# Prompt attention of a hybrid decoder step: two heads of a token block in one turn, each pair in its own half of the TensorE array

## The chip, the cores and the metric

The kernel runs on one core of one Trainium2 chip. Everything is 32-bit floating point. The metric is the device time of one execution in microseconds, from the first to the last instruction of the program and what lies around them; three executions were timed, and a further one was profiled.

## The reference, cut to what matters

Two layers, each with three token mixers side by side (a gated linear recurrence, a state-space mixer, dilated attention), a merge, and a channel mixer (dense in layer 0, eight experts in layer 1). 256 prompt tokens and 32 sample tokens go through the same weights. The change touches the prompt half of the attention: 4 heads of 64 features, three groups of projections (dilations 1, 4 and 16), whose keys lie together in one softmax.

```python
s = jnp.einsum('bnqrhd,bnkrhd->bnrhqk', qb, kb, preferred_element_type=jnp.float32) * ATT_SCALE
s = jnp.where(valid[None, :, None, None], s, -jnp.inf)
m = jnp.max(s, axis=-1, keepdims=True)
p = jnp.exp(s - m)
den = jnp.sum(p, axis=-1, keepdims=True)
o = jnp.einsum('bnrhqk,bnkrhd->bnqrhd', p, vb) / jnp.transpose(den, (0, 1, 4, 2, 3, 5))
```

So for every head and every block of 128 query tokens: scores (a contraction over 64 features), a softmax over the row, and a product of the weights with the values (64 features out).

## The kernel before, in words

Features lie on partitions, tokens in columns. TensorE is written out by hand as one long list of products; each product goes to one of eight PSUM banks, and a planning pass (`plan_mixer`) says which bank each product fills and in which order a bank is filled. `open_bank` makes TensorE wait until the bank's last content has been taken out, and `close_bank` signals that it is full. VectorE (DVE) and ScalarE (ACT) take banks out in their own hand-written orders. SyncE issues all weight and cache loads.

**Units.** The prompt attention of a layer is eight units, n = 0 to 7: unit n is head n // 2 and query block n % 2. The first block sees one block of keys, the second two. A unit goes like this:

- `scores(L, n, k)` (TensorE): for key block k three products (one for each group) of 64 partitions into bank 0. Heads 0 and 2 lie on partitions 0 to 63, heads 1 and 3 on 64 to 127.
- `prompt_scores` (DVE, from L2579): L2588 scales and masks each bank of scores into the buffer `sc`, L2591 takes the row maximum, L2592 negates it. ACT exponentiates with a running sum, DVE takes the reciprocal (L2603) and scales the row (L2604).
- `turn_weights(L, n, k)` (TensorE): three transposes of the weights into bank 2, copied out by ACT into `PT`.
- `weigh(L, n)` (TensorE): for each key block three products of 128 partitions with 64 output features, into partitions 0 to 63 or 64 to 127 of bank 4.

**Between them** stand other products of the same TensorE list. `sample_keys(L, n, k)` turns the cached keys of sample sequence n in four parts, into banks 5 and 6; DVE copies out parts 0 and 1 (L2599, L2601), ACT parts 2 and 3. `sample_scores` (one for every two sequences) needs all eight parts and runs in four column quarters of the array. `out_tile(br, m)` is one tile of the other mixers' output projections, into bank 1, taken out by DVE in `gated` (a L2284 instruction). The turning of unit n's weights and its value products stand in turn n + 1, behind the next unit's scores and key turns.

All of TensorE's products are recorded at L974 (`put`) and all of its transposes at L980 (`turn`); in the trace a product of 32-bit numbers is two records and a transpose is one. A record's shape is written partitions*columns of the loaded weights, then the output: 64*128 are the scores, 128*64 the value products, 128*32 the sample scores, 128*128 with 288 columns an `out_tile` product. ACT's instructions stand at L1838.

Of the kernel before, what the change touches and what calls it, by code (L numbers as in the profile page):

```python
# [84 lines left out]
def hybrid_decoder(nc, x_prompt, x_sample, state_hgrn, state_ssm, state_conv, cache_kv_w128, cache_kv_w512,  # L85
# [6 lines left out]
    with ctx:  # L92
# [140 lines left out]
        sc = [view(arena, 16128, 1, 384), view(arena, 16512, 2, 384)]  # L233
        PT = [view(arena, 17280, 1, 384), view(arena, 17664, 2, 384)]
# [99 lines left out]

        def plan_mixer(L):
# [79 lines left out]
            for n in range(9):  # L415
                if n < 8:
                    for k in range(n % 2 + 1):
                        job(("sc", L, n, k), 0)
                    if n == 0:
                        job(("sS", L, 0), 7)  # L420
                        job(("sS", L, 1), 3)
# [4 lines left out]
                if n > 0:  # L426
                    for k in range((n - 1) % 2 + 1):
                        job(("pt", L, n - 1, k), 2)
                    if (n - 1) % 4 == 0:
                        job(("att_o", L, (n - 1) // 4), 4)  # L430
# [525 lines left out]
        def _(pe):  # L956
# [421 lines left out]
            def weigh(L, n):  # L1378
                h, tb = n // 2, n % 2
                j, r = h // 2, 64 * (h % 2)  # L1380
                key = ("att_o", L, j)
                acc = open_bank(key) if n % 4 == 0 else psum(key)
                for k in range(tb + 1):
                    pe.wait_ge(*drained(("pt", L, n, k)))
# [6 lines left out]
                if n % 4 == 3:  # L1391
# [136 lines left out]
            def mixer(L):  # L1528
# [26 lines left out]
                for n in range(9):  # L1555
                    if n < 8:
                        scores(L, n, 0)
                        sample_keys(L, n, 0)
                        if n % 2:
                            scores(L, n, 1)  # L1560
                        sample_keys(L, n, 1)
                    if n > 0:
                        turn_weights(L, n - 1, 0)
                    if n < 8:
                        out_tile(0, n)
                        sample_keys(L, n, 2)
                        sample_keys(L, n, 3)
                        if n % 2:
                            out_tile(1, n // 2)
                    if n > 0 and n % 2 == 0:  # L1570
                        turn_weights(L, n - 1, 1)
                        sample_scores(L, n // 2 - 1)
                    if n > 0:
                        weigh(L, n - 1)
# [242 lines left out]
        def _(act):  # L1817
# [148 lines left out]
            def attention(L):  # L1966
# [5 lines left out]
                def turned_weights(m, k):  # L1972
                    key = ("pt", L, m, k)
                    copy_out(PT[m % 2][:, k, :], key, psum(key)[:, 0:384])

                for n in range(9):
                    if n < 8:
                        w = n % 2 + 1
                        act.wait_ge(*at("sc_neg", L, n + 1))
# [1075 lines left out]
```

## Time and profile before

| | us |
|---|---|
| three executions | 2180.27, 2180.68, 2182.74 (median 2180.68) |
| the profiled execution | 2180.18 |
| its span, first to last instruction | 2178.4 |
| TensorE busy (matmul) | 2137.6 (98%) |
| DVE busy | 602.9 (28%) |
| ACT busy | 376.9 (17%) |
| granted TensorE clock, mean | 0.996 |

A record's busy time runs to its modelled end. Matmul records overlap, so what an item costs on TensorE is read from its start to the start of the next item. The two layers' attention stretches run from 376.25 and from 1125.72 us of the span; the expert stage of layer 1 takes the time from about 1292 us to the end.

### The profile page before, as it was taken

What the parts mean: (1) busy time and instruction counts of PE and PEld (TensorE: products, weight loads), DVE (VectorE), ACT (ScalarE), POOL (GpSimd) and SP (SyncE); (2) the same over time, 40 slices, a digit from 0 to 9 for tenths busy, and PEclk for the clock granted to TensorE, in tenths of its full rate; (3) what the DMA queues carried; (4) which work ended last, traced back from release to release, by engine and by line L of the source; (5) the groups of instructions that cost most, each with busy time, mean ns of one, the idle gap of its engine ahead of it and who ended that gap; (6) DMA issues with size and microseconds to landing.
All of it is one profiled execution on the core that took longest, in us unless ns stands there. A gap on an engine that the chain in (4) does not pass through costs nothing.

```text
span 2178.4 us, 43348 instructions
## 1 busy us (share of the span) xinstructions
PE 2137.6 (98%) x19425; PEld 1330.8 (61%) x19425; DVE 602.9 (28%) x1181; ACT 376.9 (17%) x676; POOL 101.2 (5%) x150
## 2 busy tenths in 40 slices
PE   7999999999999999999999999999999999999998
PEld 6777777777777777777776753434343434343434
DVE  5395333443110124933244321010101010101013
ACT  3323424311000023243333030000000000000000
POOL 2001020000000000011200010000000000000001
PEclk9999999999999999999999999999999999999999
DMA  5434535684443453354464859999999999999996
GB/s 161 135 99 141 157 119 159 178 258 135 137 136 101 133 176 117 117 161 128 129 190 130 290 215 406 417 404 416 405 416 404 417 404 415 397 413 398 413 411 238
DMA packets 298648, 548.64 MB, mean 252 GB/s; under 512 B 12665, under 2 KB 229115, under 8 KB 282016
## 3 DMA queue, kind: packets, MB, share of 16 engines
q1 hardware_dynamic: 290476, 535.85, 68.3%
q10 hardware_dynamic: 6644, 5.58, 0.8%
q0 software_dynamic: 1344, 4.45, 0.5%
q8 instruction: 153, 2.51, 0.5%
q14 instruction: 31, 0.25, 0.0%
HBM read 527.15 MB, written 22.50 MB: 252 GB/s over the span
## 4 chain that ended last, share of the span: by engine, by line
PE 94%; DVE 3%; DMA 2%; ACT 1%; issue 1%; ACTq 0%; DVEq 0%
PE bank L974 92%; PE bank L980 2%; DMA mem<-in_w_moe_down_dram 1%; ACT mem L1838 1%; DVE mem L2588 0%; DVE col L2591 0%; DVE mem L2559 0%; DVE mem L2601 0%; DVE mem L2604 0%; ACTq L2148 0%; DMA hv<-in_ssm_d_dram 0%; DVE mem L2284 0%; DVE mem L2599 0%; ACT L1838 0%; DVE mem L2280 0%
## 5 line engine op out<-in xcount | busy, mean ns | idle before, releaser
L974 PE MATMUL bank<-mem 128*32 128x256 f32 (+10 forms) x11936 | 999.9, 403 | 19.2 <-DVE mem L2284 5.7
L974 PEld LDWEIGHTS bank<-mem 128*32 128x32 f32 (+3 forms) x11936 | 566.1, 121 | 434.3 <-issue 233.5
L974 PE MATMUL bank<-hflat,mem 128*128 128x288 f32 (+1 forms) x2944 | 716.6, 406 | 1.3 <-ACT hflat L1838 0.7
L974 PEld LDWEIGHTS bank<-hflat,mem 128*128 128x128 f32 (+1 forms) x2944 | 538.1, 188 | 163.3 <-issue 19.4
L1838 ACT ACTIVATE mem<-bank 128x288 f32<-128x288 f32 (+6 forms) x347 | 158.8, 463 | 802.4 <-PE bank L974 763.5
L974 PE MATMUL bank<-mem,steps 128*32 128x384 f32 (+1 forms) x3072 | 289.8, 539 | 0.0
L974 PEld LDWEIGHTS bank<-mem,steps 128*32 128x32 f32 x3072 | 95.3, 110 | 191.2 <-issue 190.3
L2284 DVE SCALAR_TENSOR_TENSOR hflat<-hflat,bank 128x512 f32<-128x512 f32 x24 | 15.1, 683 | 411.3 <-ACT hflat L1838 411.3
L1838 ACT ACTIVATE hflat<-bank 128x512 f32<-128x512 f32 (+1 forms) x40 | 19.6, 554 | 569.1 <-PE bank L974 546.2
L2284 DVE SCALAR_TENSOR_TENSOR mem<-mem,bank 128x288 f32<-128x288 f32 (+1 forms) x93 | 43.2, 479 | 214.4 <-ACT mem L1838 178.3
L1838 ACT ACTIVATE mem<-mem 128x1152 f32<-128x1152 f32 (+9 forms) x105 | 83.4, 796 | 100.1 <-DVE mem L2358 71.6
L2280 DVE TENSOR_TENSOR mem<-mem 128x1152 f32<-128x1152 f32 (+6 forms) x101 | 87.5, 867 | 7.4 <-ACT mem L1838 2.4
L980 PE MATMUL bank<-ident,mem 128*128 128x128 f32 (+3 forms) x459 | 65.2, 281 | 12.5 <-DMA mem<-in_x_sample_dram 7.4
L980 PEld LDWEIGHTS bank<-ident,mem 128*128 128x128 f32 (+3 forms) x459 | 52.6, 145 | 25.5 <-issue 12.2
L2287 DVE SCALAR_TENSOR_TENSOR mem<-mem,bank 128x384 f32<-128x384 f32 (+1 forms) x45 | 21.4, 505 | 168.0 <-PE bank L974 168.0
L1838 ACT ACT_TABLE_LOAD x41 | 52.6, 1283 | 15.3 <-issue 11.3
L930 POOL DMA_INDIRECT mem<-yslots,mem x6 | 5.9, 978 | 836.4 <-PE bank L974 834.9
L2287 DVE SCALAR_TENSOR_TENSOR hflat<-hflat,bank 128x512 f32<-128x512 f32 x24 | 15.1, 683 | 78.9 <-PE bank L974 78.9
L1838 ACT ACTIVATE hflat<-xT 128x288 f32<-128x288 f32 x24 | 10.6, 443 | 141.0 <-DVE xT L2280 86.3
L1838 ACT ACTIVATE mem<-mem,col 128x384 f32<-128x384 f32 (+2 forms) x18 | 14.7, 814 | 78.2 <-DVE col L2592 75.3
L2588 DVE SCALAR_TENSOR_TENSOR mem<-bank,amask 128x384 f32<-128x384 f32 x24 | 13.4, 558 | 50.8 <-PE bank L974 50.8
L2437 DVE SCALAR_TENSOR_TENSOR mem<-mem,vecs 128x312 f32<-128x312 f32 x48 | 26.1, 545 | 1.7
(239 smaller groups left out, 707.2 us busy)
## 6 DMA issues: line engine op xcount, KB each, us to landing
mem<-in_w_moe_up_dram SPq DMA_DIRECT2D x64, 2048.0 KB, 21.3
mem<-in_w_moe_down_dram SPq DMA_DIRECT2D x56, 2048.0 KB, 21.7
mem<-in_w_moe_up_dram SPq DMA_DIRECT2D x32, 2304.0 KB, 23.1
mem<-in_w_in_dram SPq DMA_DIRECT2D x70, 1024.0 KB, 5.2
mem<-in_w_moe_up_dram SPq DMA_DIRECT2D x16, 1536.0 KB, 22.2
mem<-in_w_ffn_up_dram SPq DMA_DIRECT2D x44, 512.0 KB, 4.8
mem<-in_cache_kv_w_dram SPq DMA_DIRECT2D x26, 512.0 KB, 4.9
mem<-in_w_ffn_down_dram SPq DMA_DIRECT2D x16, 704.0 KB, 5.1
```

What stands on the lines that cost most here:

```text
L930: return gp.indirect_dma_start(dst, None, src, bass.IndirectOffsetOnAxis(ap=slots, axis=0), bounds_check=last_row, oob_is_err=False)
L974: return mm(out, lhsT, rhs, start=start, stop=stop, skip_group_check=True)
L980: return nc.tensor.transpose(out, in_, ident[0:k, 0:k])
L1838: return nc.scalar.activation(out, in_, f, **kw)
L2280: return ve.tensor_tensor(out, a, b, op)
L2284: return ve.scalar_tensor_tensor(out, tanh, 1.0, b, ALU.add, ALU.mult)
L2287: return ve.scalar_tensor_tensor(out, a, 0.5, b, ALU.mult, op)
L2437: ins = ve.scalar_tensor_tensor(cv[:, m, 0:CW], xpad[:, m, j:j + CW], w[j], cv[:, m, 0:CW], ALU.mult, ALU.add)
L2588: empty(ve.scalar_tensor_tensor(sc[n % 2][:, k, :], psum(key)[:, 0:384], SCALE, amask[:, w - 1 - k, :], ALU.mult, ALU.add), key)
```

## The change

A turn now holds two units: two heads (n and n + 1, n even) of the same query block. Unit n is now head 2 * (n // 4) + n % 2 and query block n // 2 % 2, so that turns 0 and 4 have one key block and turns 2 and 6 have two.

- The scores of both heads are issued alternately, one on partitions 0 to 63 into bank 0, one on 64 to 127 into bank 1. Bank 1 is also that of `out_tile`.
- The turned weights go to banks 2 and 0 in alternation. `PT` and `sc` have two key blocks for both heads.
- The value products of both heads are issued alternately into the two partition halves of bank 4, one turn (two units) after their scores.
- DVE takes out both heads' scores, then makes both maxima, then the key copies, then both reciprocals and scalings. ACT's list follows.

```diff
-        sc = [view(arena, 16128, 1, 384), view(arena, 16512, 2, 384)]
-        PT = [view(arena, 17280, 1, 384), view(arena, 17664, 2, 384)]
+        sc = [view(arena, 16128 + 768 * e, 2, 384) for e in range(2)]
+        PT = [[arena[:, 17664:18048], arena[:, 18048:18432]], [arena[:, 18432:18816], over[:, 4736:5120]]]
...
+        def blocks_of(n):
+            return 1 + n // 2 % 2
+        def turns_of(n):
+            return [(e, k) for e in range(2) for k in range(blocks_of(n))]
...
+                if n < 8 and n % 2 == 0:
+                    for k in range(blocks_of(n)):
+                        for e in range(2):
+                            job(("sc", L, n + e, k), e)
...
+                    if n % 2:
+                        for i, (e, k) in enumerate(turns_of(n)):
+                            job(("pt", L, n - 1 + e, k), (2, 0)[i % 2])
...
             def scores(L, n, k):
-                h, tb = n // 2, n % 2
-                j, r = h // 2, 64 * (h % 2)
-                acc = open_bank(("sc", L, n, k))
+                j, tb = n // 4, n // 2 % 2
+                both = [open_bank(("sc", L, n + e, k)) for e in range(2)]
                 for g in range(AG):
-                    ins = put(acc[:, P * g:P * g + P], att[r:r + 64, 4 * g + j, P * tb:P * tb + P],
-                              att[r:r + 64, 4 * g + 2 + j, P * k:P * k + P])
-                close_bank(ins, ("sc", L, n, k))
+                    for e in range(2):
+                        r = slice(64 * e, 64 * e + 64)
+                        ins = put(both[e][:, P * g:P * g + P], att[r, 4 * g + j, P * tb:P * tb + P],
+                                  att[r, 4 * g + 2 + j, P * k:P * k + P])
+                        if g == AG - 1:
+                            close_bank(ins, ("sc", L, n + e, k))
...
             def weigh(L, n):
...
                     for g in range(AG):
-                        ins = put(acc[r:r + 64, P * tb:P * tb + P], kvtok[:, k, g, 256 + 64 * h:256 + 64 * h + 64],
-                                  PT[n % 2][:, k, P * g:P * g + P], k == 0 and g == 0, k == tb and g == 2)
+                        for e in range(2):
+                            v = 256 + P * j + 64 * e
+                            ins = put(acc[64 * e:64 * e + 64, P * tb:P * tb + P], kvtok[:, k, g, v:v + 64],
+                                      PT[e][k][:, P * g:P * g + P], k == 0 and g == 0, k == tb and g == 2)
...
+                for n in range(0, 8, 2):
+                    scores(L, n, 0)
+                    sample_keys(L, n, 0)
+                    if blocks_of(n) == 2:
+                        scores(L, n, 1)
+                    sample_keys(L, n, 1)
                     if n > 0:
                         sample_scores(L, n // 2 - 1)
+                        weigh(L, n - 2)
+                    out_tile(0, n)
+                    sample_keys(L, n, 2)
+                    sample_keys(L, n, 3)
+                    sample_keys(L, n + 1, 0)
+                    turn_weights(L, n, 0)
+                    sample_keys(L, n + 1, 1)
+                    if blocks_of(n) == 2:
+                        turn_weights(L, n, 1)
+                    out_tile(0, n + 1)
+                    turn_weights(L, n + 1, 0)
+                    sample_keys(L, n + 1, 2)
+                    out_tile(1, n // 2)
+                    if blocks_of(n) == 2:
+                        turn_weights(L, n + 1, 1)
+                    sample_keys(L, n + 1, 3)
+                sample_scores(L, 3)
+                weigh(L, 6)
```

On ACT a turn is now: both exponentials, the old values' bank (in turn 4), key parts 2 and 3 of sequence n, the turned weights of unit n, those of n + 1 with the key parts of sequence n + 1 between them.

TensorE, from the middle of layer 0's attention (L974 and L984 are the same line of the helper, before and after, as L980 and L990 are). Before, from the last `out_tile` of turn 1 to `weigh` of unit 1:

```order
L974 MATMUL bank<-mem 128x288 x4
L974 MATMUL bank<-mem 64x128 x3
L974 MATMUL bank<-mem 128x128 x3
L980 MATMUL bank<-ident,hflat 128x128 x6
L980 MATMUL bank<-ident,mem 128x128 x3
L974 MATMUL bank<-mem 128x288 x4
L980 MATMUL bank<-ident,hflat 128x128 x8
L980 MATMUL bank<-ident,mem 128x128 x3
L974 MATMUL bank<-mem 32x512 x4
L974 MATMUL bank<-mem 32x256 x4
L974 MATMUL bank<-mem 32x128 x4
L974 MATMUL bank<-mem 64x128 x6
```

After, the beginning of turn 2 (units 2 and 3):

```order
L990 MATMUL bank<-ident,mem 128x128 x4
L984 MATMUL bank<-mem 128x128 x6
L990 MATMUL bank<-ident,hflat 128x128 x2
L984 MATMUL bank<-mem 128x128 x6
L990 MATMUL bank<-ident,hflat 128x128 x4
L984 MATMUL bank<-mem 32x512 x4
L984 MATMUL bank<-mem 32x256 x4
L984 MATMUL bank<-mem 32x128 x4
L984 MATMUL bank<-mem 64x128 x6
L984 MATMUL bank<-mem 128x288 x4
L990 MATMUL bank<-ident,hflat 128x128 x8
L990 MATMUL bank<-ident,mem 128x128 x12
```

Scores (output 128x128 from `put`) stand as groups of six for two heads instead of groups of three for one, with two key turns between the two groups; the sample scores and the value products stand ahead of the turn's first `out_tile` instead of at its end. Within a group of six the two heads and the two banks alternate, as the diff has it.

VectorE, the second take-out of scores of layer 0. Before (unit 1's two output tiles, then unit 2):

```order
L2284 SCALAR_TENSOR_TENSOR mem<-mem,bank 128x288 x2
L2588 SCALAR_TENSOR_TENSOR mem<-bank,amask 128x384
L2591 TENSOR_REDUCE col<-mem 128x1
L2592 TENSOR_SCALAR col<-col 128x1
L2599 COPY mem<-bank 128x256
L2601 COPY mem<-bank 128x512
L2603 RECIPROCAL col<-col 128x1
L2604 TENSOR_SCALAR mem<-mem,col 128x384
L2284 SCALAR_TENSOR_TENSOR mem<-mem,bank 128x288
```

After (turn 2):

```order
L2631 SCALAR_TENSOR_TENSOR mem<-bank,amask 128x384 x4
L2636 TENSOR_REDUCE col<-mem 128x1
L2637 TENSOR_SCALAR col<-col 128x1
L2636 TENSOR_REDUCE col<-mem 128x1
L2637 TENSOR_SCALAR col<-col 128x1
L2617 COPY mem<-bank 128x256
L2619 COPY mem<-bank 128x512
L2642 RECIPROCAL col<-col 128x1
L2643 TENSOR_SCALAR mem<-mem,col 128x768
L2642 RECIPROCAL col<-col 128x1
L2643 TENSOR_SCALAR mem<-mem,col 128x768
L2314 SCALAR_TENSOR_TENSOR mem<-mem,bank 128x288
```

Four score banks are taken out in a row, and both maxima stand ahead of the key copies; the output tile's take-out stands behind both scalings.

## Rows read from the trace of the kernel before

**Rows 1.** The page: busy time by engine, and the chain that ended last.
```profile
PE 2137.6 (98%) x19425; PEld 1330.8 (61%) x19425; DVE 602.9 (28%) x1181; ACT 376.9 (17%) x676; POOL 101.2 (5%) x150
...
PE 94%; DVE 3%; DMA 2%; ACT 1%; issue 1%; ACTq 0%; DVEq 0%
```

**Rows 2.** Both attention stretches: length, busy us (x) of PE, PEld, DVE, ACT, POOL; clock; DMA.
```profile
376.25:450.11 73.86, 69.00 (x509) 52.95 (x508) 34.91 (x75) 23.37 (x46) 3.17 (x4) 1.00 0.59 169
1125.72:1199.60 73.88, 69.02 (x509) 52.94 (x508) 34.83 (x75) 23.37 (x47) 3.17 (x4) 1.00 0.59 170
```

**Rows 3.** TensorE's groups by shape in layer 0's attention.
```profile
L974 PE MATMUL bank<-mem 64*128 64x128 f32 x72 | 11.2, 289 | 1.4 <-DVE mem L2588 1.4
L974 PE MATMUL bank<-mem 128*64 128x128 f32 x72 | 9.6, 278 | 0.0
```

**Rows 4.** Timeline, weight loads around 397 us: start, us, engine, what.
```profile
397.52 1.28 PEld L974 LDWEIGHTS bank<-mem 128*64 128x64 f32 x12 [0.20 <-issue]
398.98 0.74 PEld L974 LDWEIGHTS bank<-mem 64*128 64x128 f32 x6 [0.17 <-issue]
```

**Rows 5.** Timeline of TensorE, layer 0, unit 3.
```profile
399.84 0.44 PE L980 MATMUL bank<-ident,mem 128*128 128x128 f32 x2
400.62 0.93 PE L974 MATMUL bank<-mem 64*128 64x128 f32 x6 [0.34 <-DVE mem L2588]
401.48 0.98 PE L980 MATMUL bank<-ident,mem 128*128 128x128 f32 x7
...
404.24 1.04 PE L980 MATMUL bank<-ident,mem 128*128 128x128 f32 x8
405.98 3.87 PE L974 MATMUL bank<-mem 128*128 128x288 f32 x20 [0.69 <-DVE mem L2284]
```

**Rows 6.** Timeline of TensorE: two products of 64 partitions into two banks, 203 us.
```profile
203.26 1.13 PE L974 MATMUL bank<-mem 64*128 64x512 f32 x4
...
204.32 0.22 PE L980 MATMUL bank<-ident,steps 8*128 8x8 f32 x1
```

**Rows 7.** Timeline of TensorE: products of 32 partitions on four row quarters, 2168 us.
```profile
2168.45 1.15 PE L974 MATMUL bank<-hflat,mem 32*128 32x256 f32 x16 [0.72 <-ACT hflat L1838]
2169.41 0.61 PE L974 MATMUL bank<-hflat,steps 32*128 32x256 f32 x8
```

**Rows 8.** Weight loads of products in column halves (256, then 128 columns), 286 us.
```profile
285.81 0.63 PEld L974 LDWEIGHTS bank<-mem 128*64 128x64 f32 x8 [0.39 <-issue]
...
286.61 0.19 PEld L974 LDWEIGHTS bank<-mem 32*64 32x64 f32 x4 [0.17 <-issue]
```

**Rows 9.** Who TensorE waited for in layer 0's attention: total us, times, longest.
```profile
PE bank L974 <- DVE mem L2284: 2.9, 4, 0.8
PE bank L974 <- DVE mem L2588: 1.4, 4, 0.4
PE bank L980 <- ACT mem L1838: 0.6, 1, 0.6
```

**Rows 10.** Groups of DVE and ACT in the same stretch: count, busy us, mean ns.
```profile
L2588 DVE SCALAR_TENSOR_TENSOR mem<-bank,amask 128x384 f32<-128x384 f32 x12 | 6.7, 558 | 25.2 <-PE bank L974 25.2
...
L2591 DVE TENSOR_REDUCE col<-mem 128x1 f32<-128x768 f32 x4 | 3.8, 953 | 0.1
...
L2604 DVE TENSOR_SCALAR mem<-mem,col 128x768 f32<-128x768 f32 x4 | 2.5, 620 | 0.1
...
L1838 ACT ACTIVATE mem<-bank 128x512 f32<-128x512 f32 x17 | 10.2, 597 | 4.0 <-PE bank L980 3.6
...
L1838 ACT ACTIVATE mem<-mem,col 128x768 f32<-128x768 f32 x4 | 3.7, 937 | 20.4 <-DVE col L2592 20.4
```

**Rows 11.** SyncE's queue: sequence 4's first key load, and waits in the expert stage.
```profile
387.68 0.71 SPq L656 DMA_DIRECT2D mem<-in_cache_kv_w_dram  x1
...
SPq L783 <- PE bank L974: 628.2, 153, 8.1
```

**Rows 12.** Median us from issue to landing, 365 to 470 us.
```profile
mem<-in_cache_kv_w_dram SPq DMA_DIRECT2D x13, 512.0 KB, 4.8
```

More of the change, by code:

```diff
@@ L2577, in sample_queries, with turned_keys @@
                     step(ins) if pair < 3 else say(ins, "qx_ready", L)
-            def prompt_scores(L, n):
-                w = n % 2 + 1
-                c = 4 * (n % 2)
-                for k in range(w):
-                    key = ("sc", L, n, k)
-                    dve.wait_ge(*filled(key))
-                    if n >= 2 and k == 0:
-                        for kk in range(w):
-                            dve.wait_ge(*filled(("pt", L, n - 2, kk)))
-                    empty(ve.scalar_tensor_tensor(sc[n % 2][:, k, :], psum(key)[:, 0:384], SCALE,
-                                                  amask[:, w - 1 - k, :], ALU.mult, ALU.add), key)
-                v = sc[n % 2].rearrange("p k c -> p (k c)")[:, 0:384 * w]
-                step(ve.tensor_reduce(col[:, c:c + 1], v, AX.X, ALU.max))
-                say(ve.tensor_scalar(col[:, c + 1:c + 2], col[:, c:c + 1], -1.0, None, ALU.mult), "sc_neg", L, n + 1)
+            def turned_keys(L, n):
                 if n >= 3:
@@ L2601, in prompt_scores @@
                         empty(ve.tensor_copy(KTr[n % 3][:, 256:768], psum(key)[:, :]), key)
-                dve.wait_ge(*at("sc_exp", L, n + 1))
-                step(ve.reciprocal(col[:, c + 3:c + 4], col[:, c + 2:c + 3]))
-                say(ve.tensor_scalar(v, v, col[:, c + 3:c + 4], None, ALU.mult), "sc_ready", L, n + 1)
+            def prompt_scores(L, n):
+                w = blocks_of(n)
+                for k in range(w):
+                    for e in range(2):
+                        key = ("sc", L, n + e, k)
+                        dve.wait_ge(*filled(key))
+                        if n >= 2 and k == 0:
+                            for kk in range(blocks_of(n - 2)):
+                                dve.wait_ge(*filled(("pt", L, n - 2 + e, kk)))
+                        empty(ve.scalar_tensor_tensor(sc[e][:, k, :], psum(key)[:, 0:384], SCALE,
+                                                      amask[:, w - 1 - k, :], ALU.mult, ALU.add), key)
+                rows = [sc[e].rearrange("p k c -> p (k c)")[:, 0:384 * w] for e in range(2)]
+                for e in range(2):
+                    c = 4 * e
+                    step(ve.tensor_reduce(col[:, c:c + 1], rows[e], AX.X, ALU.max))
+                    say(ve.tensor_scalar(col[:, c + 1:c + 2], col[:, c:c + 1], -1.0, None, ALU.mult), "sc_neg", L, n + e + 1)
+                turned_keys(L, n)
+                for e in range(2):
+                    c = 4 * e
+                    dve.wait_ge(*at("sc_exp", L, n + e + 1))
+                    step(ve.reciprocal(col[:, c + 3:c + 4], col[:, c + 2:c + 3]))
+                    say(ve.tensor_scalar(rows[e], rows[e], col[:, c + 3:c + 4], None, ALU.mult), "sc_ready", L, n + e + 1)
             def sample_rows(L):
@@ L2711, in mixer @@
                 for n in range(8):
-                    prompt_scores(L, n)
+                    if n % 2:
+                        turned_keys(L, n)
+                    else:
+                        prompt_scores(L, n)
                     for br, m in out_beside_scores(n):
```

96 lines of the change are left out of this document (39 added, 57 removed).

## The prediction

> **What bounds the kernel now.** I read the page first: TensorE is busy for 98% of the span and holds 94% of the chain that ended last [rows 1]. So time is won or lost in what TensorE does and in its waits. Next the two attention stretches, cut at the first scores and at the end of the last value products: 73.86 and 73.88 us, both at the full granted clock of 1.00, DVE busy for 34.9 us of them and ACT for 23.4 [rows 2]. The layers behave alike, so I work out one and double it. Then the shapes: 72 records of scores and 72 of value products a layer [rows 3], in groups of 6 and 12. The weight loads and the timeline give what a group takes, start to start: a score group of 6 takes 0.86 us (398.98 to 399.84 [rows 4, 5], and again 400.62 to 401.48 [rows 5]); 12 value records take 1.46 us (397.52 to 398.98 [rows 4]). A plain transpose record comes every 0.11 us: eight are busy for 1.04 us, of which the last one's own 0.28 us overlaps nothing [rows 3, 5]. Records of 128 columns in the other two shapes come at that pace too, and what is left over is the change of shape: 0.86 less 6 x 0.11 is 0.19 us, 1.46 less 12 x 0.11 is 0.15 us. Last the waits of TensorE [rows 9]: 4.9 us a layer by the profile's count.
>
> **The change, part by part, for one layer.**
>
> *Scores.* 12 groups of 6 records become 6 groups of 12, in which the heads alternate between row halves. If the halves run side by side a new group takes what an old one took, and six groups of 0.86 us go: 5.2 us. Whether they do, an older part of this kernel shows: two products of 64 partitions with 512 columns into two banks, four records, take 1.06 us to the next start [rows 6]. One such record alone is twice 512 columns at 2.4 GHz, 0.43 us, so four in turn need 1.71 us; side by side they need 0.85 us and a shape change. At the end of the program 16 records of 256 columns on four row quarters take 0.96 us (2168.45 to 2169.41 [rows 7]), a first-record delay included; in turn they would need 3.4 us. There four weight loads of 128 columns go with every four records in about 0.22 us, so two loads in 0.11 us, which is what the new scores need, is a rate that has been seen. Bounds: 5.2 us saved, or only the shape changes if nothing overlaps (about 1.2 us). I take 5.2.
>
> *Value products.* Four groups of 6 and four of 12 records, 4 x (0.66 + 0.15) and 4 x 1.46 us, 9.1 us, become two groups that take as long as 6 and two that take as long as 12: 4.5 us. The nearest row is another product in column halves: eight records, four of 256 and four of 128 columns, take 0.80 us (285.81 to 286.61 [rows 8]). In turn they would need 4 x 0.21 and 4 x 0.11, 1.28 us, before any shape change; in pairs 0.64 us and 0.16 for the change. Bounds again: 4.5 us saved, or 0.6 if nothing overlaps. I take 4.5.
>
> *Returns to full-array work.* Six returns from scores to transposes are gone, and the first interval after each was about 0.05 us long: 0.3 us. Fewer returns from values to an output tile give or take as little.
>
> These three are 10.0 us a layer.
>
> *Waits that go.* Before, TensorE waits four times a layer for the first key block's scores to be taken out before it may write the second block's, as both are in bank 0: 399.84 to 400.62 is 0.78 us for two transposes that need 0.22 and the shape change 0.15, so 0.4 us, four times, 1.7 us [rows 5]. And four times for DVE to empty bank 1 before the second output tile: 404.24 to 405.98 is 1.74 us for work of 0.88, 0.86 us, four times, 3.5 us [rows 5]. With one 0.9 us at the end for ACT the waits come to 6.1 us; the profile's 4.9 [rows 9] is less because a record's own end hides the first tenths of each.
>
> *Waits that come.* I walked the three engines through each turn with the durations of [rows 10]. (a) The first output tile of a layer now finds bank 1 full of scores until DVE has done both take-outs: 0.7 us. (b) The second key block's scores wait for two take-outs of 0.56 us in a row instead of one: the last record's end and a reaction of 0.4 us, then 1.15 us, against 0.6 us of key turns: 1.05 us, but only in turns 2 and 6, so 2.1 us. (c) Right behind key parts 2 and 3 of the turn's first sequence come those of the second, into the same two banks, and ACT copies them out (0.60 us each) only behind two exponentials: 0.5 us in turns 2, 4 and 6, and 0.6 in turn 0, 2.2 us with the small second parts. (d) The next turn's scores wait for ACT's or DVE's last take-out of banks 0 and 1: 0.3 us, three times, 0.9 us. (e) The last sample scores need all key parts, the last of which ACT now copies last: 0.95 us. The bank-1 wait of 0.86 us is almost gone, 0.05 each. Sum: 7.1 us. DVE (34.9 us of work) and ACT (23.4 us) stay below the new stretch of some 65 us, so neither becomes the bound; the twelve take-outs, the maxima (0.95 us) and scalings (0.62 us) are as many as before.
>
> *Moved past a queue.* SyncE loads the next keys when part 3 of an older sequence has been turned. Part 3 of sequence 1 used to be reached at about 387 us and sequence 4's load started at 387.68 [rows 11]; now it is reached near 388 us. Loads land 4.8 us after their issue in the median [rows 12], the first ones later, as they queue behind each other, and sequence 4 is used near 406 us. Closest is sequence 3, all issued before 387.68 and wanted near 398 us. I cost this at nothing; without this cover it would be the lateness itself, 1 or 2 us in a layer.
>
> *What it carries to.* Behind both stretches stands TensorE-bound work. In the expert stage SyncE waits 628 us in total, 153 times, for TensorE to free a slab [rows 11], so the loads run as TensorE lets them, and their start shifts with layer 1's attention. Nothing is given back later.
>
> *Sum.* 10.0 - (7.1 - 6.1) = 9.0 us a layer, 18.0 us in all. Against the profiled execution (2180.18 us, 1.8 more than its span) that is 2162.2; the median of the runs is 0.5 higher, so I say **2162.7 us**. No change can be told from one of 0.2%, 4.4 us.
>
> **A page that speaks against it.** The rows show full overlap for pairs and fours [rows 6 to 8]. The Trainium skill, TensorE: Matmul & The Clock Gate, part "Packing small matmuls — row/col tiling", lists measured speedups of 3.07 for four row tiles and 2.38 for three column tiles, some 78% of the full factor, and says that weight loads overlap running products only when the row groups differ, which column halves don't. By its 78% a pair would cost 1.29 times as much; no run here has shown that so far.
>
> **The rivals.**
>
> 1. *Pairs overlap in part.* A weight load isn't hidden in each pair. For: the 1.06 us of [rows 6] are 0.21 more than full overlap; I read them as a shape change and a first load, but if they are a loss of each pair, a pair costs 1.25 of what it should. 0.25 x 0.11 us x 72 pairs is 2.0 us a layer: 2166.7. Against: [rows 7] show records of four quarters at full pace. 5%. The Trainium skill's factor, on the same page and part, would make it 2.3 us a layer and 2167.3.
> 2. *One kind of pair doesn't overlap at all.* Scores (36 pairs x 0.11 = 4.0 us a layer) or values (as much): 2170.7. Against: [rows 6] for rows, [rows 8] for columns. 12% for the two together. Both: 2178.6, no change; the change then doesn't do what it says; 3%.
> 3. *The turn is bound by ACT and DVE.* Two heads' exponentials of 0.94 us and two scalings stand between scores and transposes, key copies behind them. If the waits are 3 us a layer more than I walked: 2168.7. For: the walk's margins are a few tenths at eight places. 7%.
> 4. *Slower: alternating between halves is itself a change of shape.* TensorE drains each time the half changes, at 0.15 us as between groups. 72 alternations a layer, no overlap: 72 x 0.15 = 10.8 us come, only 2.0 of shape changes between groups go, waits plus 1.0: 9.8 us a layer slower, 2200.3. It decides against the change from about 0.015 us an alternation if nothing overlaps. Against: the 0.96 us of [rows 7] have no room for it. 3%.
>
> **How the numbers follow.** The forecast has 70%. It is 2162.7, give or take 2 us a layer for the walked waits and for instruction fetches that fall elsewhere: 2158.7 to 2166.7. Rivals 1 and 3 (12%) reach 2168.7; the cases beyond it are 18%. Range 2158.7 to 2169.0. Faster by over 0.2% are all but the last of rival 2 and rival 4: 0.94; within 0.2%: 0.03; slower: 0.03.
>
> **What would show it.** Still 72 records each of 64*128 and 128*64 in a stretch, but their busy time near 6 and 5 us instead of 11.2 and 9.6, as overlapping records count once. A score group of twelve at 0.86 us from its start to the next. The stretches at about 65 us. TensorE's waits for DVE's score take-out longer each but fewer, those for L2284 nearly gone, more for ACT. The expert stage as long as before. It would be wrong if twelve score records took 1.5 us, if a stretch stayed above 70 us, or if 18 us went in the stretches and came back in the expert stage as waits for slabs.

## The result, and the profile after

| | before | after |
|---|---|---|
| median of six executions each (lowest to highest) | 2181.76 us (2180.27 to 2186.07) | 2165.78 us (2162.74 to 2170.40) |
| the profiled execution | 2180.18 us | 2166.27 us |
| its span | 2178.4 us | 2164.5 us |
| its mean granted clock | 0.996 | 0.994 |

The ratio is 0.9926, with a 95% interval of 0.9912 to 0.9940: the change makes the kernel some 16 us faster. The forecast was 2162.7 us (2158.7 to 2169.0), and faster.

The page, busy time by engine and the chain that ended last, beside [rows 1]:

```profile
PE 2122.2 (98%) x19425; PEld 1353.8 (63%) x19425; DVE 602.9 (28%) x1181; ACT 376.9 (17%) x676; POOL 101.2 (5%) x150
...
PE 96%; DVE 1%; ACT 1%; issue 1%; ACTq 0%; DMA 0%; DVEq 0%
```

TensorE has as many records as before and is busy 15.4 us less. DVE and ACT do exactly what they did. DVE's share of the chain falls from 3% to 1%. In layer 0's attention stretch alone it held about a quarter of the chain and now holds some 7%, and ACT's share there rises from 1% to 6%. Most of DMA's 2% went back to one wait of 2.4 us for expert weights at 2155 us of before, which the change's profile doesn't have.

Both attention stretches, cut as in [rows 2] but to the first product behind the last value product (columns: length, busy us of PE, PEld, DVE, ACT, POOL, clock, DMA share, GB/s). With that cut the stretches of before are 73.95 and 74.06 us.

```profile
376.05:441.54 65.49, 60.15 (x509) 45.38 (x508) 35.02 (x75) 23.37 (x46) 3.17 (x4) 1.00 0.65 189
1114.76:1180.24 65.48, 60.14 (x510) 45.39 (x509) 35.01 (x75) 23.37 (x46) 3.18 (x4) 1.00 0.65 188
```

So 8.46 and 8.58 us go, 17.0 together, at the same granted clock. TensorE's groups in layer 0's stretch, beside [rows 3]:

```profile
L984 PE MATMUL bank<-mem 64*128 64x128 f32 x72 | 5.6, 287 | 2.7 <-DVE mem L2631 2.0 <-DVE mem L2314 0.5 <-ACT mem L1861 0.2
L984 PE MATMUL bank<-mem 128*64 128x128 f32 x72 | 4.8, 278 | 0.0
```

The count and the mean duration of one record are those of before (289 and 278 ns), the busy times are half: 11.2 to 5.6, 9.6 to 4.8. Two records side by side count once. That is what overlap looks like in this view. The timeline has the same, in layer 0 from turn 1's end into turn 2, beside [rows 5]:

```profile
387.80 0.60 PE L990 MATMUL bank<-ident,mem 128*128 128x128 f32 x4
388.67 0.94 PE L984 MATMUL bank<-mem 64*128 64x128 f32 x12 [0.27 <-DVE mem L2314]
389.54 0.44 PE L990 MATMUL bank<-ident,hflat 128*128 128x128 f32 x2
390.96 0.94 PE L984 MATMUL bank<-mem 64*128 64x128 f32 x12 [0.98 <-DVE mem L2631]
391.83 0.66 PE L990 MATMUL bank<-ident,hflat 128*128 128x128 f32 x4
...
436.39 0.93 PE L990 MATMUL bank<-ident,mem 128*128 128x128 f32 x7
438.25 9.38 PE L984 MATMUL bank<-mem 128*32 128x512 f32 x96 [0.92 <-ACT mem L1861]
```

Twelve score records take 0.87 us to the next start (388.67 to 389.54), where six took 0.86. Between the two score groups TensorE has two transposes and then idles: 389.54 to 390.96 is 1.42 us. The weight loads show the value products, beside [rows 4]: twelve take 0.81 us (394.06 to 394.87), 24 take 1.46 (408.93 to 410.39).

```profile
394.06 0.63 PEld L984 LDWEIGHTS bank<-mem 128*64 128x64 f32 x12 [0.20 <-issue]
394.87 1.75 PEld L984 LDWEIGHTS bank<-mem 128*128 128x128 f32 x8 [0.17 <-issue]
...
408.93 1.29 PEld L984 LDWEIGHTS bank<-mem 128*64 128x64 f32 x24 [0.20 <-issue]
410.39 1.27 PEld L984 LDWEIGHTS bank<-mem 128*128 128x128 f32 x6 [0.17 <-issue]
```

And who TensorE waited for, beside [rows 9]:

```profile
PE bank L984 <- DVE mem L2631: 2.6, 3, 1.0
PE bank L984 <- ACT mem L1861: 1.1, 2, 0.9
PE bank L990 <- ACT mem L1861: 1.0, 3, 0.3
PE bank L984 <- DVE mem L2314: 0.5, 2, 0.3
```

The four waits of up to 0.8 us for DVE's output tile are gone; those that are left of L2314 are two of 0.3 ahead of scores. Nobody waits for a DMA. In their place stand fewer, longer waits for the score take-outs and new ones for ACT's copies.

**Layer 0 summed.** Each record of TensorE from its start to the next start, grouped by the record's shape. All waits of TensorE in this stretch stand behind a transpose, so they fall into the last row.

| shape | before, us | after, us | change | forecast |
|---|---|---|---|---|
| scores, 64*128 | 10.35 | 5.22 | -5.13 | -5.2 |
| value products, 128*64 | 9.01 | 4.53 | -4.48 | -4.5 |
| output tiles, 128*128 with 288 columns | 24.06 | 24.07 | 0.0 | 0 |
| sample scores, 128*32 | 6.77 | 6.79 | 0.0 | 0 |
| transposes and the waits behind them | 23.76 | 24.90 | +1.14 | +0.7 |
| sum | 73.95 | 65.51 | -8.44 | -9.0 |

**Outside the stretches** the executions differ. The three parts are between the layers' attention, from layer 1's attention to the first product of the expert stage, and that stage to the end. First before, then after:

```profile
450.20:1125.72 675.52, 670.87 (x3789) 518.04 (x3788) 217.26 (x396) 145.43 (x251) 34.41 (x34) 1.00 0.49 145
1199.78:1292.28 92.50, 87.86 (x777) 67.35 (x777) 35.13 (x113) 18.82 (x37) 3.17 (x4) 0.96 0.70 246
1292.28:2178.39 886.11, 877.39 (x11601) 361.88 (x11601) 102.99 (x185) 33.72 (x70) 11.78 (x12) 0.99 0.99 397
```

```profile
441.54:1114.76 673.22, 669.29 (x3791) 517.14 (x3789) 217.22 (x396) 145.42 (x251) 34.40 (x34) 1.00 0.49 146
1180.24:1279.06 98.82, 93.05 (x778) 70.87 (x777) 35.12 (x113) 18.82 (x37) 3.17 (x4) 0.91 0.68 232
1279.06:2164.51 885.45, 876.89 (x11601) 398.01 (x11601) 103.02 (x185) 33.73 (x70) 11.77 (x12) 1.00 0.99 397
```

The expert stage is as long as before (885.5 and 886.1 us). The middle part is 6.3 us longer at a clock of 0.91 instead of 0.96, the first 2.3 us shorter. Together the three parts take 3.4 us of the 17.0 back in this execution. Whether the 6.3 us belong to the change is a question for the experiments. What they are made of, the timeline shows:

```profile
1193.75 1.71 PE L984 MATMUL bank<-mem 128*32 128x256 f32 x48
1195.39 1.06 PE L984 MATMUL bank<-tmask,mem 128*128 128x8 f32 x8
1196.38 0.40 PE L984 MATMUL bank<-mem 128*32 128x256 f32 x1
1197.83 2.24 PE L984 MATMUL bank<-mem 128*32 128x256 f32 x47 [1.05 <-issue]
1200.00 1.88 PE L984 MATMUL bank<-tmask,mem 128*128 128x8 f32 x8
1201.81 3.22 PE L984 MATMUL bank<-mem 128*32 128x256 f32 x48
```

After a gap of 1.05 us in which TensorE waited for nothing that the profile shows, the same 48 products take 3.22 us instead of 1.71. The granted clock says why:

```profile
1186.00:1199.00 13.00, 11.95 (x181) 9.49 (x183) 2.29 (x4) 1.74 (x4) 2.37 (x3) 1.00 1.12 280
1199.00:1205.70 6.70, 6.70 (x81) 4.86 (x70) 1.24 (x2) 0.00 (x0) 0.00 (x0) 0.50 1.09 362
```

From 1199.0 to 1205.7 us the granted clock is 0.50, the level of 1.2 GHz, with TensorE busy throughout, ahead of the fall but for that gap too. In the whole middle part 17.1 us lie at that level, against 6.9 in before. As the same products take about twice as long there (3.22 us for 1.71), an estimate is 5.1 us for the clock and 1.05 for the gap: nearly all of the 6.3.

### The profile page after: what moved, and what is told of

Its sections match the earlier page's. It is cut to its first block, busy times and chain, and to the rows that moved or that the text cites. A ratio compares the mean times of both kernels' runs of the same rounds, so it can differ in the third digit from the quotient of the medians.

```text
span 2164.5 us, 43368 instructions
## 1 busy us (share of the span) xinstructions
PE 2122.2 (98%) x19425; PEld 1353.8 (63%) x19425; DVE 602.9 (28%) x1181; ACT 376.9 (17%) x676; POOL 101.2 (5%) x150
## 4 chain that ended last, share of the span: by engine, by line
PE 96%; DVE 1%; ACT 1%; issue 1%; ACTq 0%; DMA 0%; DVEq 0%
PE bank L984 93%; PE bank L990 3%; ACT mem L1861 1%; DVE mem L2589 0%; DVE mem L2631 0%; ACTq L2178 0%; DMA hv<-in_ssm_d_dram 0%; ACT hflat L1861 0%; ACT L1861 0%; DVE mem L2310 0%; ACTq L2181 0%; DVE hflat L2310 0%; DVE mem L2314 0%; DVE mem L2950 0%; ACTq L2183 0%
## 5 line engine op out<-in xcount | busy, mean ns | idle before, releaser
L984 PE MATMUL bank<-mem 128*32 128x256 f32 (+10 forms) x11936 | 982.5, 403 | 19.4 <-issue 7.8
L984 PEld LDWEIGHTS bank<-mem 128*32 128x32 f32 (+4 forms) x11936 | 580.5, 121 | 402.1 <-issue 225.9
L984 PE MATMUL bank<-hflat,mem 128*128 128x288 f32 (+1 forms) x2944 | 716.6, 406 | 1.3 <-ACT hflat L1861 0.7
L984 PEld LDWEIGHTS bank<-hflat,mem 128*128 128x128 f32 (+1 forms) x2944 | 538.1, 188 | 163.3 <-issue 19.4
L984 PE MATMUL bank<-mem,steps 128*32 128x384 f32 (+1 forms) x3072 | 289.9, 539 | 0.0
L984 PEld LDWEIGHTS bank<-mem,steps 128*32 128x32 f32 x3072 | 102.3, 110 | 184.3 <-issue 181.4
L2314 DVE SCALAR_TENSOR_TENSOR hflat<-hflat,bank 128x512 f32<-128x512 f32 x24 | 15.1, 683 | 410.4 <-ACT hflat L1861 410.4
L2314 DVE SCALAR_TENSOR_TENSOR mem<-mem,bank 128x288 f32<-128x288 f32 (+1 forms) x93 | 43.2, 479 | 225.4 <-ACT mem L1861 178.6
L990 PE MATMUL bank<-ident,mem 128*128 128x128 f32 (+3 forms) x459 | 64.6, 279 | 13.0 <-DMA mem<-in_x_sample_dram 7.3
L990 PEld LDWEIGHTS bank<-ident,mem 128*128 128x128 f32 (+3 forms) x459 | 52.7, 143 | 27.5 <-issue 11.8
L2310 DVE TENSOR_TENSOR mem<-mem,bank 128x512 f32<-128x512 f32 (+1 forms) x40 | 23.5, 587 | 9.6 <-PE bank L984 8.7
```

The costliest lines, as they stand in the source:

```text
L984: return mm(out, lhsT, rhs, start=start, stop=stop, skip_group_check=True)
L990: return nc.tensor.transpose(out, in_, ident[0:k, 0:k])
L2310: return ve.tensor_tensor(out, a, b, op)
L2314: return ve.scalar_tensor_tensor(out, tanh, 1.0, b, ALU.add, ALU.mult)
```

## The experiments

Two theories were put to the chip. The first is the sum of the prediction: the gain is 72 + 72 records that run two at a time, less waits that can be walked. The second is that the rearrangement of the turns (fewer changes of shape, other waits) brings a good part of it, and the alternation little. In the expectations these are theories A and C; theory B is that the halves overlap whatever the order inside a group. Beside them stood the open question whether the time behind layer 1's attention is the change's.

The first four kernels below ran on one chip with seven executions of before (median 2184.51 us), the next four on another with 13 (2183.05 us), the last three on a third with 11 (2183.74 us). Stretches are cut as above, and the change's are 65.49 us.

**The change again.** No edit.

> The change itself once more, for comparison on the same chip. Both stretches 65.5 us again, as they are set by fixed orders. If the loss outside the stretches (6.3 us behind layer 1's attention in the profiled execution) belongs to the change, it is there again at the same place; if it is a clock drop that falls in some executions, the place and the size differ.

Measured: 2163.55 us (2160.94 to 2164.17), ratio 0.9910 [0.9888, 0.9933]. The stretches are 65.49 and 65.49 us. The three parts outside them:

```profile
441.77:1116.35 674.58, 670.93 (x3791) 518.23 (x3789) 217.20 (x396) 145.30 (x251) 34.36 (x34) 1.00 0.49 145
1181.84:1274.76 92.92, 88.19 (x779) 68.13 (x778) 35.09 (x113) 18.82 (x37) 3.16 (x4) 0.96 0.71 247
1274.76:2161.81 887.05, 878.67 (x11601) 586.12 (x11601) 103.01 (x185) 33.70 (x70) 11.75 (x12) 1.00 0.99 397
```

The middle part is 92.92 us at 0.96, within 0.4 us of before. The 98.82 us were one execution's and not the change's. What they follow is the time at the half clock. In the ten profiles of this document in which this part is the same work, it is 90.8 to 91.5 us long with 3.4 us at that level, 92.5 to 94.0 with 6.8, 94.1 and 95.5 with 10.2, 96.0 with 13.8, and 98.8 with 17.1: roughly half a microsecond for each.

**The two heads' scores one after the other** instead of alternately; all else as in the change.

```diff
-                for g in range(AG):
-                    for e in range(2):
+                for e in range(2):
+                    for g in range(AG):
```

> Only the order of the score products changes: head by head instead of alternating; turns, banks and waits stay as in the change. Theory A (the gain comes from pairs that run side by side, and TensorE takes its list in order): a score group of twelve records takes about 1.4 us instead of 0.87, six groups a layer, so each attention stretch grows from 65.5 to about 68.7 us and the time by 6 us over the change. Theory B (each half has a queue of its own, so the order inside a group doesn't matter): 0.9 us a group and no difference. Theory C (the gain is the regrouping into turns and fewer changes of shape, the pairs give little): no difference either, and the same in the run with both kinds apart.

Measured: 2166.44 us (2165.34 to 2168.82), ratio 0.9929 [0.9906, 0.9951]; both stretches 66.40 us, 0.91 a layer more than the change. The price that follows from "in turn is not side by side" was 3.2 us a layer. The timeline at the place quoted above:

```profile
388.72 1.23 PE L984 MATMUL bank<-mem 64*128 64x128 f32 x12 [0.27 <-DVE mem L2314]
389.89 0.44 PE L990 MATMUL bank<-ident,hflat 128*128 128x128 f32 x2
391.02 1.23 PE L984 MATMUL bank<-mem 64*128 64x128 f32 x12 [0.69 <-DVE mem L2631]
```

A group takes 1.17 us, not 0.87, and not the 1.50 of twelve in turn (measured below). The single records of the first group show how: the first head's start at 376.11, .32, .43, .54 us and so on, the second head's first one at 376.44, beside the first head's third (376.43) and ahead of its fourth. TensorE had gone on to the other half 0.33 us after the start, with half of the first head's records still to come. So the halves overlap without alternation, three records of six. Theory A took the list to run in order and is wrong in that; theory B would have had no loss. Half of what is left of the price comes back: the first head's bank is full 0.3 us ahead of the second's, and DVE starts its take-outs 1.00 us after the group's first record in both kernels (388.72 to 389.72 here, 388.67 to 389.67 in the change). So DVE is that much further when the group ends, and the three waits for L2631 shrink by 0.3 us each (2.6 to 1.7 us in the view of waits). Six groups of 0.3 us more, less three waits of 0.3 us less, are the 0.9 us.

**The value products head by head**, the same edit in `weigh`.

```diff
-                    for g in range(AG):
-                        for e in range(2):
+                    for e in range(2):
+                        for g in range(AG):
```

> Only the order of the value products changes: head by head within a key block. Theory A: 24 records take about 2.6 us instead of 1.35, 12 take 1.3 instead of 0.8; 36 records a layer are no longer hidden, less what overlaps where one head's records end and the other's begin: each stretch about 3.5 us longer, the time 7 us over the change. Theories B and C: no difference.

Measured: 2167.32 us (2163.19 to 2169.16), ratio 0.9924 [0.9901, 0.9948]; stretches 66.56 and 66.57 us, 1.07 a layer more. Twelve value products now take 1.08 us instead of 0.81:

```profile
394.15 0.90 PEld L984 LDWEIGHTS bank<-mem 128*64 128x64 f32 x12 [0.20 <-issue]
395.23 1.75 PEld L984 LDWEIGHTS bank<-mem 128*128 128x128 f32 x8 [0.17 <-issue]
```

Column halves behave as row halves do: overlap in part when in turn. So the price is 1.07 us a layer and not the 3.5 that was expected.

**Both head by head.**

> Both orders head by head: what is left of the change is the turn of two heads, the banks and the fewer changes of shape. Theory A: the two losses add, stretches of about 72 us, 1 to 2 us a layer below the kernel before (changes of shape 2.0 us less, waits 1.0 us more), the time 2 to 5 us below before. Theory C: about as fast as the change, 14 to 18 us below before.

Measured: 2167.30 us (2165.12 to 2169.49), ratio 0.9933 [0.9909, 0.9956]; stretches 67.48 and 67.47 us, 1.98 a layer more, which is 0.91 + 1.07. The two parts add up, and nothing behind them takes it back. The expectations stood at some 72 us for the first theory and 65.5 for the second, and 67.5 is neither: as the halves overlap in any order, this kernel can't tell what the overlap is worth. The next one can. The medians of these three kernels lie 2.9 to 3.8 us above the change's, where the stretches say 1.8, 2.1 and 4.0. Differences of 2 us are seen in a stretch and not in a median of four.

**Both heads in one half.** Both heads' scores from partitions 0 to 63, both heads' value products into partitions 0 to 63, same order, same counts, same banks, so that nothing can lie side by side. The second head's own scores and its own half of the output are left out, so the kernel's outputs are other numbers.

```diff
-                        r = slice(64 * e, 64 * e + 64)
+                        r = slice(0, 64)
...
-                            ins = put(acc[64 * e:64 * e + 64, P * tb:P * tb + P], kvtok[:, k, g, v:v + 64],
+                            ins = put(acc[0:64, P * tb:P * tb + P], kvtok[:, k, g, v:v + 64],
```

> Scores of both heads are computed from partitions 0 to 63 and both heads' value products go to partitions 0 to 63, so no two records can run side by side; the outputs of the prompt attention are other numbers. All else is the change. Theory A (the gain is in records that run side by side): a score group of twelve takes 0.87 + 0.67, about 1.5 us, 24 value records 2.7 us instead of 1.4; each stretch 7 to 8 us longer than 65.5, that is about 73, and the time at 2176 to 2179, close to the kernel before. Theory C (regrouping alone gives most of it): stretches under 69 us.

Measured: 2182.83 us (2177.24 to 2185.57, ten executions), ratio to before 0.9997 [0.9986, 1.0007]: no difference that can be told. The groups of layer 0, the timeline and the two stretches:

```profile
L984 PE MATMUL bank<-mem 64*128 64x128 f32 x72 | 9.5, 279 | 2.3 <-DVE mem L2631 1.6 <-DVE mem L2314 0.5 <-ACT mem L1861 0.2
L984 PE MATMUL bank<-mem 128*64 128x128 f32 x72 | 8.7, 276 | 0.0
```

```profile
389.33 1.57 PE L984 MATMUL bank<-mem 64*128 64x128 f32 x12 [0.27 <-DVE mem L2314]
390.83 0.44 PE L990 MATMUL bank<-ident,hflat 128*128 128x128 f32 x2
```

```profile
376.26:450.56 74.30, 69.56 (x509) 53.55 (x509) 36.27 (x77) 23.36 (x47) 3.16 (x4) 0.98 0.58 169
1125.00:1200.85 75.85, 71.09 (x509) 54.89 (x508) 36.26 (x77) 23.35 (x46) 3.16 (x4) 0.95 0.58 168
```

Twelve score records take 1.50 us. The stretches have half-clock spells of 3.4 and 6.8 us in them, which shows in the clock column (0.98 and 0.95). Less half of each spell they are 72.6 and 72.4 us, an estimate of what they would be without: 1.4 and 1.6 us below before, 7 us above the change. The second theory falls. Of the 8.5 us a layer the rearrangement alone brings about 1.5, and records side by side the other 7. That the time as a whole shows nothing of those 1.5 fits the clock: the ten executions have a median mean clock of 0.9925 and the 13 of before 0.995, which by an estimate is 5.5 us.

**A smaller wait: the key turns ahead of the second score group.** In turns 2 and 6 TensorE has two key turns, then the second score group, and waits 0.98 us there by the view. Here all six stand ahead of it: the two, and the four of the next part.

```diff
                     sample_keys(L, n, 0)
+                    sample_keys(L, n, 1)
                     if blocks_of(n) == 2:
                         scores(L, n, 1)
-                    sample_keys(L, n, 1)
```

> In a turn the second part of the key turns stands ahead of the second group of scores instead of behind it. If the second group waits for VectorE's two take-outs (0.98 us after other work has run out), 0.44 us of transposes fill half of that wait, in turns 2 and 6 of each layer: stretches 0.9 to 1.0 us shorter, about 64.5, the time 2 us less. If the wait only moves to the next item: no difference.

Measured: 2160.38 us (2159.04 to 2161.94), ratio 0.9892 [0.9874, 0.9910]; stretches 64.32 and 64.32 us, 1.17 a layer less than the change, and the wait is 0.55 instead of 0.98:

```profile
389.65 0.87 PE L990 MATMUL bank<-ident,hflat 128*128 128x128 f32 x6
391.08 5.53 PE L984 MATMUL bank<-mem 64*128 64x128 f32 x56 [0.55 <-DVE mem L2631]
```

From the end of the first score group to the second group is 1.43 us, as in the change, but six transposes lie in it instead of two. So the wait was DVE's, and its time can be filled. The four transposes save more than the 0.44 us that they last: from the first one behind the first score group to the sample scores it is 2.88 us in the change (389.54 to 392.42) and about 2.3 here, as one change of shape is gone too. Two such places are the 1.17 us.

**The last value products ahead of the last sample scores**, which wait 0.92 us for ACT's last key copy.

```diff
-                sample_scores(L, 3)
                 weigh(L, 6)
+                sample_scores(L, 3)
```

> At the end of the attention the last value products stand ahead of the last sample scores. The wait of 0.92 us for ScalarE's copy of the last keys should be covered by them: the stretch up to the first output tile behind is 0.6 us shorter (the values wait a little for the last turned weights). If the sample softmax behind it, which starts from the sample scores, is close, its wait of up to 1 us appears ahead of the turning of the sample weights and takes it back.

Measured: 2164.79 us (2164.00 to 2165.68), ratio 0.9914 [0.9897, 0.9931]. The stretch has another end now, so the first 288-column product behind it is taken as the mark: it comes 73.95 us after the first scores in the change (376.05 to 450.00) and 73.45 us here (376.42 to 449.87). Half a microsecond a layer of 0.9 is kept, since a new wait comes right behind:

```profile
446.84 1.05 PE L984 MATMUL bank<-ident,mem 128*128 128x128 f32 x8
448.13 1.90 PE L984 MATMUL bank<-ident,mem 128*128 128x128 f32 x12 [0.24 <-DVE mem L2314]
```

**Both moves, and the first turned weights ahead of the other sequence's keys.**

```diff
-                    sample_keys(L, n + 1, 0)
                     turn_weights(L, n, 0)
+                    sample_keys(L, n + 1, 0)
```

> Both moves together, and the turned weights of a turn's first head ahead of the next sequence's first keys, which wait for ScalarE. Expected: 1.5 to 1.8 us less in each layer, about 63.8 us a stretch, and 3 us in all against the change: 2160 to 2163 median, unless the half clock takes it.

Measured: 2160.39 us (2159.06 to 2163.32), ratio 0.9896 [0.9876, 0.9915]. The mark comes at 72.29 us (376.34 to 448.63), 1.66 a layer before the change's. The waits of its layer 0:

```profile
PE bank L984 <- DVE mem L2631: 1.7, 3, 0.6
PE bank L984 <- DVE mem L2314: 0.8, 3, 0.3
PE bank L990 <- DVE mem L2643: 0.6, 2, 0.3
PE bank L984 <- ACT mem L1861: 0.2, 1, 0.2
PE bank L990 <- ACT mem L1861: 0.2, 1, 0.2
```

ACT's waits are nearly gone, and the turned weights now wait for DVE's scaling (L2643), 0.3 us twice: the 1.17 of the first move and the 0.50 of the second are the whole 1.66, so the third brought nothing.

**The change, the first move and all three, on one chip**, since the medians so far came from different chips.

> The change unaltered, a third time, beside the two next kernels on one chip. Theory (the sum over the attention stretches): both stretches 65.5 us again, time 2162 to 2167, whatever of it above 2162 stands as half-clock spells and issue gaps outside the stretches. Rival (the 98.8 us behind layer 1's attention that the first profile showed belong to the change): that part is above 96 us again instead of 92.5 to 93.

> The key turns ahead of the second score group, again. By its profile each stretch is 1.17 us shorter than the change's, so 2.3 us less in time than the change on this chip. Rival: the 3 us and more by which its median lay below the change's before were the chip and the scatter, and the medians now differ by less than 1 us.

> All three moves, again. By the start of the items behind the attention 1.66 us a layer less than the change: 3.3 us in time, 1.0 less than the key turns alone. Rival: what the two further moves take out of the attention comes back as the wait for DVE's output tile behind it and elsewhere, and the time equals that of the key turns alone within 0.5 us.

| | us | ratio to before | first stretch | behind layer 1's attention |
|---|---|---|---|---|
| the change | 2165.00 (2164.71 to 2170.07) | 0.9927 [0.9914, 0.9940] | 65.48 | 94.06 |
| key turns ahead | 2162.23 (2159.89 to 2163.97) | 0.9909 [0.9896, 0.9922] | 64.31 | 91.45 |
| all three moves | 2161.25 (2157.31 to 2163.96) | 0.9906 [0.9892, 0.9921] | another cut | another cut |

The key turns ahead are 2.8 us faster than the change in the medians, and their slowest execution lies below its fastest; the stretches said 2.3. Both that version and the one with all three moves beat the change and before. Between these two, the 1.0 us of the medians is what the marks say and less than the scatter: it is left open. The stretches of one kernel repeat to 0.01 us from chip to chip, and the part behind layer 1's attention was 98.8, 92.9 and 94.1 us in three profiles of the same kernel.

## Why the prediction was right

**Scores and values: right, to a tenth.** The sum had 5.2 and 4.5 us a layer; the table shows 5.13 and 4.48. Six groups of 0.87 us are left of twelve of 0.86. The rows it rested on, four records of 64 partitions into two banks and 16 on row quarters [rows 6, 7], were the right ones: the 1.06 us of [rows 6] were a shape change and a first load and no loss of each pair. Taking off the 0.19 us of a shape change, twelve records take 0.68 us on two halves and 1.31 on one. That is a factor of 1.93; with the change of shape left in it is 1.72. The Trainium skill, TensorE: Matmul & The Clock Gate, part "Packing small matmuls — row/col tiling", lists speedups for three and four tiles of 512 columns; an estimate for a pair from the 78% of full that they come to is 1.56. The trace doesn't agree for pairs of 128 columns by either count, and rival 1, which gave each pair a loss of a quarter, is out. So are rivals 2 and 4: both kinds overlap, and an alternation costs nothing that can be seen.

**Where the gain comes from: right.** The prediction gave 8.0 of 10.0 us to records hidden side by side and shape changes the rest, less 1.0 for waits. With nothing side by side 7 of the 8.5 us of a layer are lost (an estimate, with half of the half-clock spells taken off), and the kernel's time can't be told from that of before.

**Waits.** The walk through each turn, place by place, in layer 0 (from start to start, less 0.11 us for a transpose, or 0.20 ahead of a change of shape):

| | forecast | measured |
|---|---|---|
| gone: bank 0, four; bank 1, four; ACT, one | 6.1 | 6.0 |
| (a) first output tile, and bank 1 afterwards | 0.7 + 0.2 | 0.8 + 0.15 |
| (b) second score group, turns 2 and 6 | 2.1 | 2.1 |
| (c) key turns behind ACT | 2.2 | 2.1 |
| (d) the next turn's scores | 0.9 | 1.0 |
| (e) last sample scores | 0.95 | 1.0 |

The view of waits has only 5.2 us for the same places, as it had 4.9 for 6.1 before: a record's own end hides the first tenths of each. Rival 3, in which DVE or ACT becomes the bound, is out by the same table.

**The part that was off** is the smallest: "Six returns from scores to transposes are gone, and the first interval after each was about 0.05 us long: 0.3 us." They are gone, and at that price: what these first intervals take above 0.11 us came to 0.66 us for twelve of them before and comes to 0.33 for six now. But six other intervals of 0.05 to 0.06 us over have come in their place, three right behind the waits for ACT's copies and three a few transposes further on (398.26, 413.80, 430.18 and 398.89, 414.43, 430.81 us). What all transposes take above 0.11 us each (0.20 ahead of a change of shape) and above the waits of the table was 0.70 us before and is 0.66 now, so the term brought next to nothing. That and 0.15 us in the balance of the waits are most of the difference between 9.0 forecast and 8.46 measured in layer 0.

**The load queue, and what it carries to: right.** Sequence 4's first key load now starts later, at 388.43 us instead of 387.68 [rows 11], near the 388 that was named, and no wait for a DMA appears in the stretch. The expert stage, 885.5 to 887.3 us in three profiles of the change against 886.1, gives nothing back. That TensorE sets its pace, as the prediction had it, shows in the records: from the 400th to the 8,800th of the stage, before, the change and the change again keep the same distances to 0.1 us. What differs lies at the ends of the stage. Before has 8.9 us at the half clock and the wait of 2.4 us for expert weights there, the first profile of the change has neither, but 2 us of gaps in which TensorE waited for nothing that the profile shows.

**The absolute time.** 2162.7 us was forecast and 2165.78 measured, with before at 2181.76 instead of 2180.68 in the larger sample. In differences of medians: 18.0 forecast; 16.0, 21.0 and 18.7 us in the three sets of executions. The stretches say 17.0 in every profile. What lies between is outside them: 3.4 us more than before in the first profile, 0.4 and 2.1 in the two others. The prediction allowed 2 us a layer for walked waits and instruction fetches; the waits needed 0.15 us of it, and the parts outside needed most in the first profile. There the half clock carries it: 17.1 us of it behind layer 1's attention against 6.9. What sets these spells and the gaps stays open: no run aimed at them. So the mechanism and its size in the stretches were forecast; how close the time itself came is in part the luck of the clock, which moves it by as much as the miss of 3.1 us.

## What to carry to other kernels

Products that use half of the array's rows or columns are worth pairing with their twins: for records of 128 columns the second of a pair costs nothing, and more than half of the new waits here (4 of 7.15 us a layer) are those that come when two heads' results need two banks at once, which can be walked with durations of the old trace to a tenth of a microsecond. Then look for work that is free of those waits and put it into them; here one line moved brought another 2.3 us. Judge steps of 1 or 2 us by the length of the stretch they are in, which repeats to 0.01 us, and not by the time of the whole, which scatters by 3 to 9 from the lowest to the highest execution of one kernel.

## What the runs showed of the hardware that was not expected

- **Halves overlap without alternation.** With six records for one half and then six for the other, the other half starts 0.33 us after the first, beside its third record and ahead of its fourth, fifth and sixth: twelve take 1.17 us, against 0.87 alternating and 1.50 in one half. So TensorE doesn't hold a record for a free half back until the last one for a busy half has begun; the seventh of the list starts 0.11 us ahead of the fourth. Column halves do the same: six and six take 1.08 us, against 0.81 alternating. Whether it would reach further ahead than over three records was not tried.
- **Half-clock spells have a fixed price, and favoured places.** On one core the granted clock falls to 0.50, mostly for 3.4 or 6.8 us, three to seven times an execution. In three profiles of the change 23.9, 16.2 and 20.5 us of the span lay at that level. In the expert stage a spell of 3.4 us puts the records behind it back by 1.66 us (before against the change, from the 400th record to the 8,800th), and the part behind layer 1's attention is longer by half of the time at that level (the run of the change again). The places recur, but not all in each execution: in 12 of the 13 profiles one spell begins 63 to 70 us behind the end of layer 1's attention. Inside an attention stretch a spell fell only in the kernel with both heads in one half. The mean clock alone doesn't give the time: of the eleven last executions of before, the two at 0.998 took 2178.5 and 2178.84 us, the one at 0.992 took 2184.95, but one at 0.995 took 2185.18.
